# One constant product in place of three, and the second residual moved ahead of the second tile's gate, at the end of a feed-forward

## The chip, the cores and the metric

The kernel runs on one core of a Trainium2 chip. The metric is device microseconds of one execution; the lower, the better. The kernel before took 1181.12 us (median of three runs, 1177.47 to 1183.35).

## The reference

Two transformer blocks run one after the other on 256 rows of 1024 numbers, all in float32. The first block has two layers (an even and an odd one). In each, after the mixer:

```
h = x * (1.0 + sc_f) + sh_f
y = conv_ffn(h, w_up, conv_w, w_down)           # silu(gate) * val, 2816 wide
x = layer_norm(DN_ALPHA * x + (1.0 + g_f) * y, ln_ffn_g, ln_ffn_b)
```

`sc_f`, `sh_f` and `g_f` come from a second input `c` by a product with `ada_w`. The layer after it begins with `h = x * (1 + sc_m) + sh_m` and a product with its input weights. The second block (RMS norms, three attentions, a feed-forward 4096 wide) begins with `rmsnorm(x)` and a product with `w_in_2`.

The change lies at the two places where a feed-forward of the first block ends and the next layer begins. They are called turns here: the first turn (after feed-forward 0, towards the odd layer) and the second turn (after feed-forward 1, towards the second block).

## The kernel before, in words

The 256 rows are two tiles of 128 rows (`tt` 0 and 1); `x[:, tt, :]` is 128 x 1024. Every product of float32 matrices is made of three products of rounded parts (`product`, lines 1287 to 1289: high by high, high by low, low by high). The high part of a weight unit is made by ScalarE (`hi_unit`, line 849), the low part by GpSimd (`lo_unit`, line 733), and SyncE loads the next weights when a low part has been made.

The output of a feed-forward lies in four PSUM banks, 128 x 512 each: banks 0 and 1 are the two column halves of tile 0, banks 2 and 3 those of tile 1. TensorE finishes them in this order: the last three blocks' products of tile 0, then those of tile 1 (`downward` with `(0,)` and then `(1,)`).

VectorE has one queue, worked off in the order written. At the end of `ffn(f)` (lines 2237 to 2267) it does four kinds of work on each bank `j`:

- `gated(j)`, line 2249: multiply the bank by the gate row. It waits for bank `j` to be full; `gated(3)` waits for `down_done`, TensorE's very last product of the feed-forward.
- the residual, line 2261: `x = ALPHA * x + bank`; it needs its own `gated(j)` (`link.need(mark)`).
- the statistic of these 512 columns, line 2007 (`chunk_statistics`), and after the second bank of a tile `bn_aggr` (line 2267), which gives `var_ready` to GpSimd for the reciprocal square root (`power`, lines 745 and 747).

The order written is gated(0), gated(1), residual 0, statistic 0, gated(2), residual 1, statistic 1, aggregate of tile 0, gated(3), residual 2, statistic 2, residual 3, statistic 3, aggregate of tile 1.

First turn, after that. VectorE normalizes tile 0 (line 2029), builds eight columns of modulation from a bank of TensorE (`mod_columns`, lines 1942 to 1951), and normalizes tile 1. TensorE has meanwhile made 32 products of one column each (`mod_columns`, line 1486), waited for `gate_copied`, and run `keep_warm(3, 4)` (line 1395): three products of constants, 128 x 512, whose result nobody reads. In the trace each such float32 product is two records. Then it transposes x, eight blocks of tile 0 and eight of tile 1 (`transpose_rows`, line 1468; it waits for each tile's normalization). Bank `q` of the transposed x is full when both tiles' blocks `2q` and `2q+1` are in. ScalarE (line 892) and VectorE (line 1979) read it out into `h`, GpSimd makes most of the low part (line 772), and TensorE goes on with `first_units(2, ...)` (line 1424) and `second_unit` (line 1387).

Second turn. TensorE runs `keep_warm(11)`. VectorE does a whole layer norm (lines 2018 and 2021), ScalarE sums squares (line 1202), GpSimd raises to the power, VectorE scales (line 2058), and TensorE transposes `xn` and starts `first_units(4, ...)` (line 1425).

Of the kernel before, what the change touches and what calls it, by code (L numbers as in the profile page):

```python
# [108 lines left out]
def build(nc, W, consts, out):  # L109
# [156 lines left out]
    with ctx:  # L266
# [175 lines left out]
        def full(eng, name):  # L442

            b, _, k = turns[name]
            eng.wait_ge(bank_full[b], k)
            return bank[b]

        def evacuated(eng, name):

            b, k, _ = turns[name]  # L450
            eng.wait_ge(bank_free[b], k + 1)

        def free(name):

            return bank_free[turns[name][0]]
# [818 lines left out]
        def _(pe):  # L1274
# [117 lines left out]
            def keep_warm(n, b=6):  # L1392

                for _ in range(n):
                    nc.tensor.matmul(bank[b][:, :], ident, cst[:, 0:512], start=True, stop=True)
# [13 lines left out]
            def first_units(n, gs, rows=False, low_last=False):  # L1409
# [17 lines left out]
                def final(part, mm):  # L1427
                    g, _, w, i = part
                    if i == (TT if rows else w // P) - 1:
                        mm.then_inc(bank_full[4 + g % 2], 1)  # L1430
# [29 lines left out]
            def transpose_rows(n, src, ready=None):  # L1460

                o = [begin(("ht", n, q)) for q in range(4)]
                for tt in range(TT):
                    if ready is not None:
                        pe.wait_ge(row_ready, ready + tt)
                    for kt in range(KD):
                        c = S * (kt % 2) + P * tt
                        mm = nc.tensor.transpose(o[kt // 2][:, c:c + P], src[:, tt, P * kt:P * (kt + 1)], ident)
                        if tt == 1 and kt % 2 == 1:
                            done(mm, ("ht", n, kt // 2))  # L1470
# [238 lines left out]
            ffn(0)  # L1709
            mod_columns(1, (0,))  # L1710
            pe.wait_ge(gate_copied, 2)
            keep_warm(3, 4)
            transpose_rows(2, x, 3)
            first_units(2, G_Z[:1], rows=True)
            second_unit(G_Z[1], rows=True)
# [196 lines left out]
        def _(dve):  # L1912
# [92 lines left out]
            def chunk_statistics(tt, i, n):  # L2005

                return V.bn_stats(bnst[:, tt, 6 * i:6 * i + 6], x[:, tt, n * i:n * (i + 1)])
# [154 lines left out]
            def ffn(f, after_block=None):  # L2162
# [73 lines left out]
                def product_full(j):  # L2236

                    if j < 3:
                        full(dve, ("acc", f, j))
                    else:  # L2240
                        dve.wait_ge(down_done, d0 + nb)
                    return bank[j]

                def gated(j):

                    o = product_full(j)
                    if j < 2:
                        dve.wait_ge(gate_copied, 2 * f + j + 1)
                    return link.mark(V.tensor_tensor(o[:, :], o[:, :], grow[:, 1, 512 * (j % 2):512 * (j % 2 + 1)], ALU.mult))
# [6 lines left out]
                mark = gated(0)  # L2256
                for j, (tt, i) in enumerate(chunks):
                    c, o = slice(512 * i, 512 * (i + 1)), bank[j]
                    after = gated(j + 1) if j < 3 else None
                    link.need(mark)  # L2260
                    V.scalar_tensor_tensor(x[:, tt, c], x[:, tt, c], ALPHA, o[:, :], ALU.mult, ALU.add
                                           ).then_inc(free(("acc", f, j)), 1)
                    mark = after
                    evacuated(dve, ("acc", f, j))
                    link(chunk_statistics(tt, i, 512))
                    if i:
                        V.bn_aggr(mv[:, tt, :], bnst[:, tt, 0:12]).then_inc(var_ready, 1)


            dve.wait_ge(cond_exp, 1)  # L2270
# [95 lines left out]
            mod_columns(0, (1,), (0, 0))  # L2366
            h_columns(1, modT[:, 0, 24:32], modT[:, 0, 16:24])
            ffn(0, lambda b: restore_rows(1, 0, (b,)))
            normalize_rows(("ffn", 0), 1, (0,))
            mod_columns(1, (0,), (2, 0))  # L2370
# [59 lines left out]
            mod_columns(1, (1,), (0, 1))  # L2430
            h_columns(3, modT[:, 1, 24:32], modT[:, 1, 16:24])
            ffn(1, lambda b: restore_rows(3, 2, (b,)))
            layer_norm(("ffn", 1), 3)
            rms_rows(("rms",), D ** 0.5)
# [57 lines left out]
            rms_rows(("out2",), 1.0)  # L2492
            h_columns(5, mlp_gain, None)
            ffn(2)
            dve.wait_ge(ln_in, 32 * 4 + 16)
            for j in range(4):
# [33 lines left out]
```

## Time and profile before

| | |
|---|---|
| median of three runs | 1181.12 us |
| the profiled execution's own time | 1176.84 us |
| its span | 1175.0 us |
| TensorE busy | 1126.1 us (96%) |
| VectorE, ScalarE, GpSimd busy | 539.2, 590.9, 832.3 us |
| mean granted TensorE clock | 0.985 |
| `keep_warm`, line 1395 | 40 records, 372.6 to 981.0 us |
| `gated`, line 2249 | 8 instructions; idle before them 5.4 us in 4 waits for TensorE |

The busy times are sums over the whole span. The turns are short stretches: the first from some 363 to 392 us, the second from some 668 to 696 us. A row of the timeline gives start, length, engine, line and operation, what is written and read, and in square brackets the idle time of that engine before it and who ended it. Rows of one kind are merged: "x16" is sixteen of them, and the length is that of all.

### The profile page before, as it was taken

What the parts mean: (1) busy time and instruction counts of PE and PEld (TensorE: products, weight loads), DVE (VectorE), ACT (ScalarE), POOL (GpSimd) and SP (SyncE); (2) the same over time, 40 slices, a digit from 0 to 9 for tenths busy, and PEclk for the clock granted to TensorE, in tenths of its full rate; (3) what the DMA queues carried; (4) which work ended last, traced back from release to release, by engine and by line L of the source; (5) the groups of instructions that cost most, each with busy time, mean ns of one, the idle gap of its engine ahead of it and who ended that gap; (6) DMA issues with size and microseconds to landing.
All of it is one profiled execution on the core that took longest, in us unless ns stands there. A gap on an engine that the chain in (4) does not pass through costs nothing.

```text
span 1175.0 us, 21678 instructions
## 1 busy us (share of the span) xinstructions
PE 1126.1 (96%) x8119; PEld 1030.3 (88%) x8119; DVE 539.2 (46%) x1120; ACT 590.9 (50%) x894; POOL 832.3 (71%) x297
## 2 busy tenths in 40 slices
PE   5899999999999989999999989999999999999997
PEld 2799898999997978899999878999999988999996
DVE  4668877865656675783223441333111333111112
ACT  0455435454543564455545444555776543555444
POOL 3567569988785635888888746556656776988884
PEclk9899989999998999999999999999999999999999
DMA  9987798999985445697656315444444544666652
GB/s 337 320 270 205 249 289 276 337 321 327 308 294 188 133 126 181 188 292 217 195 171 204 108 46 181 133 128 130 139 144 144 190 151 144 204 190 186 189 180 88
DMA packets 253484, 238.03 MB, mean 203 GB/s; under 512 B 18075, under 2 KB 216528, under 8 KB 253424
## 3 DMA queue, kind: packets, MB, share of 16 engines
q1 hardware_dynamic: 235104, 198.70, 54.9%
q10 hardware_dynamic: 17712, 38.28, 9.1%
q8 instruction: 41, 0.67, 0.2%
q0 software_dynamic: 608, 0.22, 0.1%
q14 instruction: 19, 0.16, 0.0%
HBM read 236.12 MB, written 1.05 MB: 202 GB/s over the span
## 4 chain that ended last, share of the span: by engine, by line
PE 71%; DMA 8%; POOL 6%; ACT 6%; DVE 5%; issue 3%; SPq 1%; ACTq 0%; POOLq 0%; DVEq 0%
PE bank L1287 17%; PE bank L1288 17%; PE bank L1289 17%; POOL unit_lo L733 5%; PE bank L1312 3%; PE bank L1321 3%; PE bank L1313 2%; ACT unit_hi L849 2%; DMA raw<-in_ffn_w_up 2%; PE bank L1425 2%; DMA ada<-in_ada_w 1%; PE bank L1528 1%; PE bank L1348 1%; DMA raw<-in_ev_w_in 1%; DVE x L2044 1%
## 5 line engine op out<-in xcount | busy, mean ns | idle before, releaser
L733 POOL TENSOR_TENSOR unit_lo<-raw,unit_hi 128x2048 fp32r<-128x2048 f32 (+5 forms) x87 | 343.7, 3955 | 220.0 <-ACT unit_hi L849 219.2
L1287 PE MATMUL bank<-h_hi,unit_hi 128*128 128x256 f32 x1152 | 327.0, 284 | 0.0
L1288 PE MATMUL bank<-h_lo,unit_hi 128*128 128x256 f32 x1152 | 325.9, 283 | 0.0
L1289 PE MATMUL bank<-h_hi,unit_lo 128*128 128x256 f32 x1152 | 325.9, 283 | 0.0
L784 POOL TENSOR_TENSOR unit_lo<-raw,unit_hi 128x2048 fp32r<-128x2048 f32 (+1 forms) x70 | 257.0, 3672 | 75.1 <-ACT unit_hi L998 65.5
L1287 PEld LDWEIGHTS bank<-h_hi,unit_hi 128*128 128x128 f32 x1152 | 220.7, 192 | 5.3 <-issue 2.5
L1288 PEld LDWEIGHTS bank<-h_lo,unit_hi 128*128 128x128 f32 x1152 | 220.8, 192 | 2.5
L1289 PEld LDWEIGHTS bank<-h_hi,unit_lo 128*128 128x128 f32 x1152 | 220.8, 192 | 0.0
L849 ACT ACTIVATE unit_hi<-raw 128x2048 fp32r<-128x2048 f32 (+5 forms) x97 | 161.3, 1664 | 103.5 <-DMA raw<-in_ffn_w_up 27.3
L787 POOL TENSOR_TENSOR down<-raw_down,down 128x1024 fp32r<-128x1024 f32 x70 | 176.0, 2515 | 0.2 <-ACT down L1024 0.2
L2177 DVE SCALAR_TENSOR_TENSOR work<-bank,cols,work 128x254 f32<-128x254 f32 (+1 forms) x176 | 72.6, 473 | 129.3 <-ACT work L985 129.3
L1287 PE MATMUL bank<-down,y_hi 128*128 128x512 f32 x296 | 116.7, 394 | 3.5 <-DVE y_lo L2209 2.2
L1288 PE MATMUL bank<-down,y_hi 128*128 128x512 f32 x296 | 116.0, 392 | 0.0
L1289 PE MATMUL bank<-down,y_lo 128*128 128x512 f32 x296 | 115.3, 389 | 0.0
L998 ACT ACTIVATE unit_hi<-raw 128x2048 fp32r<-128x2048 f32 (+1 forms) x60 | 90.9, 1514 | 7.0 <-DMA raw<-in_ffn_w_up 6.0
L983 ACT ACTIVATE work<-bank,cols 128x256 f32<-128x256 f32 x44 | 20.8, 473 | 118.1 <-PE bank L1289 101.3
L2206 DVE TENSOR_TENSOR bank<-bank,work 128x256 f32<-128x256 f32 x32 | 13.8, 432 | 133.9 <-ACT work L988 133.9
L1024 ACT ACTIVATE down<-raw_down 128x1024 fp32r<-128x1024 f32 x60 | 63.4, 1056 | 14.4 <-PE bank L1289 14.3
L1312 PE MATMUL bank<-h_hi,unit_hi 128*128 128x256 f32 x272 | 69.7, 293 | 0.0
L1287 PEld LDWEIGHTS bank<-down,y_hi 128*128 128x128 f32 x296 | 55.8, 189 | 14.6 <-issue 4.9
L1313 PE MATMUL bank<-h_lo,unit_hi 128*128 128x256 f32 x272 | 67.8, 286 | 0.0
L1289 PEld LDWEIGHTS bank<-down,y_lo 128*128 128x128 f32 x296 | 55.6, 188 | 12.2
(363 smaller groups left out, 2180.4 us busy)
## 6 DMA issues: line engine op xcount, KB each, us to landing
raw<-in_ffn_w_up SPq DMA_DIRECT2D x86, 512.0 KB, 5.2
raw<-in_w_in SPq DMA_DIRECT2D x60, 512.0 KB, 4.6
raw_down<-in_ffn_w_down SPq DMA_DIRECT2D x44, 512.0 KB, 5.6
ada<-in_ada_w ACTq DMA_DIRECT2D x16, 1024.0 KB, 7.1
raw<-in_w_up SPq DMA_DIRECT2D x64, 256.0 KB, 3.1
raw_down<-in_w_down SPq DMA_DIRECT2D x32, 512.0 KB, 3.5
raw<-in_ev_w_in SPq DMA_DIRECT2D x28, 512.0 KB, 5.3
att<-in_ada_w ACTq DMA_DIRECT2D x14, 1024.0 KB, 8.0
```

The lines of the kernel that those rows point to most:

```text
L733: nc.gpsimd.tensor_tensor(ul[g % 2][:, w], raw_home(g)[:, w], uh[g % 2][:, w].bitcast(F32), ALU.subtract).then_inc(lo_up, 1)
L784: nc.gpsimd.tensor_tensor(ul[s][:, 0:w], raw[s][:, 0:w], uh[s][:, 0:w].bitcast(F32), ALU.subtract).then_inc(lo_up, 1)
L787: nc.gpsimd.tensor_tensor(down[:, 1 - k, 1, :], rawd[1 - k][:, :], down[:, 1 - k, 0, :].bitcast(F32), ALU.subtract).then_inc(lo_dn, 1)
L849: nc.scalar.activation(uh[s][:, w], raw_home(g)[:, w], ACT.Copy).then_inc(hi_up, 1)
L998: nc.scalar.activation(uh[s][:, 0:w], raw[s][:, 0:w], ACT.Copy).then_inc(hi_up, 1)
L1024: nc.scalar.activation(down[:, 1 - k, 0, :], rawd[1 - k][:, :], ACT.Copy).then_inc(hi_dn, 1)
L1287: nc.tensor.matmul(o, sh, mh, start=first, stop=False)
L1288: nc.tensor.matmul(o, sh, ml, start=False, stop=False)
L1289: return nc.tensor.matmul(o, sl, mh, start=False, stop=last)
L1312: nc.tensor.matmul(o[:, 0:S], uh[s][:, a], mh[:, kt, :], start=kt == 0, stop=False)
L1313: nc.tensor.matmul(o[:, 0:S], uh[s][:, a], ml[:, kt, :], start=False, stop=False)
L2177: return V.scalar_tensor_tensor(t[:, back:S], bank[4 + s][:, S * j:S * (j + 1) - back], w, t[:, back:S], ALU.mult, ALU.add)
```

## The change

Two edits. In `ffn` the product `gated(2)` is issued after the aggregate of tile 0 and not before residual 1, and `gated(3)` directly behind it. The order becomes gated(0), gated(1), residual 0, statistic 0, residual 1, statistic 1, aggregate of tile 0, gated(2), gated(3), residual 2, statistic 2, residual 3, statistic 3, aggregate of tile 1. This holds for both turns. In the first turn `keep_warm` runs one product of constants and not three.

```diff
@@ -1709,7 +1709,7 @@
             ffn(0)
             mod_columns(1, (0,))
             pe.wait_ge(gate_copied, 2)
-            keep_warm(3, 4)
+            keep_warm(1, 4)
             transpose_rows(2, x, 3)
             first_units(2, G_Z[:1], rows=True)
             second_unit(G_Z[1], rows=True)
@@ -2256,7 +2256,7 @@
                 mark = gated(0)
                 for j, (tt, i) in enumerate(chunks):
                     c, o = slice(512 * i, 512 * (i + 1)), bank[j]
-                    after = gated(j + 1) if j < 3 else None
+                    after = gated(j + 1) if j % 2 == 0 else None
                     link.need(mark)
                     V.scalar_tensor_tensor(x[:, tt, c], x[:, tt, c], ALPHA, o[:, :], ALU.mult, ALU.add
                                            ).then_inc(free(("acc", f, j)), 1)
@@ -2265,6 +2265,8 @@
                     link(chunk_statistics(tt, i, 512))
                     if i:
                         V.bn_aggr(mv[:, tt, :], bnst[:, tt, 0:12]).then_inc(var_ready, 1)
+                    if j == 1:
+                        mark = gated(2)
```

## Rows read from the trace of the kernel before

**Rows 1.** The page's chain that ended last, shares by engine.
```profile
PE 71%; DMA 8%; POOL 6%; ACT 6%; DVE 5%; issue 3%; SPq 1%; ACTq 0%; POOLq 0%; DVEq 0%
```

**Rows 2.** Timeline, VectorE, first turn: start, length, engine, line, operation, [idle before].
```profile
363.78 1.39 DVE L2249 TENSOR_TENSOR bank<-bank,gate_rows 128x512 f32<-128x512 f32 x2 [1.23 <-PE bank L1289]
...
365.79 0.69 DVE L2007 BATCH_NORM_STATS2 small<-x 128x6 f32<-128x512 f32 x1
367.96 0.70 DVE L2249 TENSOR_TENSOR bank<-bank,gate_rows 128x512 f32<-128x512 f32 x1 [1.48 <-PE bank L1289]
368.57 0.68 DVE L2261 SCALAR_TENSOR_TENSOR x<-x,bank 128x512 f32<-128x512 f32 x1
...
370.13 0.67 DVE L2249 TENSOR_TENSOR bank<-bank,gate_rows 128x512 f32<-128x512 f32 x1
370.72 0.67 DVE L2261 SCALAR_TENSOR_TENSOR x<-x,bank 128x512 f32<-128x512 f32 x1
...
375.32 0.81 DVE L2029 TENSOR_SCALAR x<-x,small 128x1024 f32<-128x1024 f32 x1 [0.18 <-POOL small L747]
```

**Rows 3.** Timeline, first turn: TensorE, then ScalarE, then GpSimd.
```profile
368.37 4.42 PE L1486 MATMUL bank<-consts,accg 128*128 128x1 f32 x32
372.65 5.38 PE L1395 MATMUL bank<-consts 128*128 128x512 f32 x6
377.88 1.91 PE L1468 MATMUL bank<-consts,x 128*128 128x128 f32 x16
...
385.74 1.22 PE L1424 MATMUL bank<-unit_hi,h_lo 128*128 128x256 f32 x8 [0.48 <-POOL h_lo L772]
...
379.23 1.02 ACT L892 ACTIVATE h_hi<-bank,cols 128x256 fp32r<-128x256 f32 x2 [13.74 <-PE bank L1468]
...
381.44 4.25 POOL L772 TENSOR_TENSOR h_lo<-h_full,h_hi 128x512 fp32r<-128x512 f32 x3 [6.23 <-DVE h_full L1979]
```

**Rows 4.** Stretches of 1 us, first turn; third number from the end: granted clock.
```profile
371.00:372.00 1.00, 1.00 (x6) 1.00 (x7) 0.96 (x2) 0.00 (x0) 0.18 (x1) 0.50 0.56 79
...
377.00:378.00 1.00, 1.00 (x4) 0.35 (x3) 0.00 (x0) 0.00 (x0) 0.00 (x0) 0.59 0.00 0
```

**Rows 5.** The odd mixer's end, without constant products: the timeline's transposes.
```profile
476.82 3.59 PE L1468 MATMUL bank<-consts,x 128*128 128x128 f32 x16 [0.21 <-DVE x L2029]
```

**Rows 6.** The same place: a stretch of 1 us with its granted clock.
```profile
480.00:481.00 1.00, 0.41 (x3) 0.06 (x1) 0.93 (x4) 0.29 (x1) 0.38 (x1) 0.89 1.08 371
```

**Rows 7.** Timeline, second turn: VectorE, then TensorE.
```profile
672.89 0.70 DVE L2249 TENSOR_TENSOR bank<-bank,gate_rows 128x512 f32<-128x512 f32 x1 [1.48 <-PE bank L1289]
...
684.29 0.75 DVE L2058 TENSOR_SCALAR att<-x,small 128x1024 f32<-128x1024 f32 x1 [0.53 <-POOL small L747]
...
685.92 0.75 DVE L2058 TENSOR_SCALAR att<-x,small 128x1024 f32<-128x1024 f32 x1 [0.87 <-POOL small L747]
...
673.30 9.60 PE L1395 MATMUL bank<-consts 128*128 128x512 f32 x22
...
685.20 3.51 PE L1468 MATMUL bank<-consts,att 128*128 128x128 f32 x16 [2.29 <-DVE att L2058]
```

**Rows 8.** Stretches of 1 us, second turn, with the granted clock.
```profile
685.00:686.00 1.00, 0.80 (x4) 0.83 (x5) 0.13 (x2) 0.00 (x0) 0.77 (x2) 0.51 0.00 0
...
688.00:689.00 1.00, 1.00 (x8) 1.00 (x8) 0.40 (x1) 1.00 (x4) 0.00 (x0) 0.78 0.00 0
```

**Rows 9.** Timeline, TensorE, the turn of the second block's output product.
```profile
983.13 1.09 PE L1468 MATMUL bank<-consts,att 128*128 128x128 f32 x8 [0.24 <-DVE att L2058]
985.75 0.36 PE L1425 MATMUL bank<-h_hi,unit_hi 128*128 128x256 f32 x1 [1.53 <-ACT h_hi L890]
```

**Rows 10.** The stretch of 1 us in which it stands idle there.
```profile
984.00:985.00 1.00, 0.22 (x3) 0.00 (x0) 0.40 (x1) 1.00 (x4) 1.00 (x1) 1.00 0.14 49
```

**Rows 11.** The chain that ended last, in order of time: start, length, what.
```profile
386.96 5.76 PE bank L1387 x48
...
462.62 0.37 SPq L665
463.03 5.30 DMA raw<-in_ffn_w_up
```

## Prediction

> **What bounds the kernel now.** I read the page first, for the chain that ended last: TensorE is 71% of it and VectorE 5% [rows 1], so an edit on VectorE pays only where TensorE waits for it, and one on TensorE pays wherever it sits. Then I read the timeline of each turn engine by engine, and the granted clock in stretches of 1 us.
>
> In the first turn VectorE stands idle 1.48 us before gated(2), waiting for bank 2, though residual 1 behind it in the queue needs nothing more [rows 2]. From there it runs without a real gap to the second normalization, which ends at 375.32 + 0.81 = 376.13. TensorE is later than that: its constant products run from 372.65 to about 377.88, and the transposes start on their heels [rows 3]. So in the first turn the constant products are the bound, by 1.75 us against x of tile 1 (377.88 - 376.13), and by more against tile 0. The clock explains why they are so long. The granted clock is 0.50 (1.2 GHz) from 371 us on, 2.6 us into the one-column products, and comes back to 2.4 GHz at about 377.8 (0.59 granted over 377 to 378) [rows 4]. Six records took 377.88 - 372.65 = 5.23 us, 0.872 each; at 2.4 GHz it is 9.60 / 22 = 0.436 [rows 3, 7].
>
> In the second turn TensorE has long finished its constant products (673.30 + 9.60 = 682.90) and waits 2.29 us for VectorE's scaled tile [rows 7]. There VectorE and its helpers are the bound, and the 1.48 us gap stands in front of their whole chain.
>
> **Edit 1, VectorE's order.** Nothing is added or removed, two products move. Before: the first statistic ends at 365.79 + 0.69 = 366.48, and residual 2 starts at 370.72, 4.24 us later [rows 2]. After: residual 1, statistic 1 and aggregate run at once; they take 370.13 - 368.57 = 1.56 us start to start, so from 366.51 to 368.07. Bank 2 was there at 367.96, so gated(2) doesn't wait. gated(3) follows; TensorE has gone on to its one-column products at 368.37 [rows 3], so bank 3 is full too, and two gates take 1.39 us less the 0.09 by which a residual starts inside the gate before it (367.96 + 0.70 against 368.57), 1.30 us; gated(3) comes at about 368.72 and doesn't wait either. Residual 2 starts at 368.07 + 1.30 = 369.37. **VectorE is 370.72 - 369.37 = 1.35 us earlier**, with everything behind it: second normalization done at 374.78. What is moved past what: gated(2) now stands behind statistic 1, which costs bank 2 about 0.1 us; nobody else waits for bank 2. GpSimd gets tile 0's variance some 2 us sooner, and nobody uses it before VectorE's own turn comes.
>
> In the first turn, as it stands, this edit alone would pay nothing, since TensorE comes later. With edit 2 it is a cover: see below.
>
> In the second turn the pattern repeats, gated(2) again idle 1.48 [rows 7], so the scaled tiles are ready at 684.29 + 0.75 - 1.35 = 683.69 and at 685.92 + 0.75 - 1.35 = 685.32. Transposes then start at 683.85 and not at 685.20. What follows hangs on the clock, which had fallen by 685 (0.51 granted) after 2.1 us of idleness, and was back near 688.4 (0.78 over that microsecond) [rows 8]. Lower bound: it falls again. Sixteen transposes at 3.51 / 16 = 0.219 us end at 687.36, then 1.08 us of products at half rate lose 0.54: the gain is 1.35 - 0.54 = 0.8. Upper bound: with TensorE idle for only 0.95 us (682.90 to 683.85) and 0.6 us between the tiles, the clock stays at 2.4 GHz, as it does over 1.53 us of idleness in another turn [rows 9, 10]. Then transposes take 1.09 / 8 = 0.136 at most, tile 1's run from 685.48 to about 686.5, and products start at 686.4 against 688.46: 2.05. I take **1.35**, near the middle; a low value and a high value are both one step of the clock away.
>
> **Edit 2, one constant product.** Four of six records go. If the clock runs as it did (half rate until 377.8), TensorE is through its constants at 372.65 + 2 x 0.872 = 374.4. Tile 0 is normalized by then, since VectorE is already at tile 1's normalization (375.32 - 1.35 = 373.97). Eight transposes at 0.219 end at 376.15, tile 1 has been ready since 374.78, eight more end at 377.9. Bank 0 is full after the tenth, at 374.4 + 2.19 = 376.6; before it was 377.88 + 10 x 0.119 = 379.07, and ScalarE started 0.16 us behind it [rows 3]. VectorE's first read waits for the twelfth transpose: 377.03 against 379.31, 2.28 earlier. GpSimd's three low parts hang on those reads, and TensorE waits 0.48 us for the last of them [rows 3]. From the earlier start of both (2.47 and 2.28), less a tenth or two for a bank that now comes in steps of 0.44 us, I take **2.15 us for the first turn**. Upper bound: the four records themselves, 3.5 us, if nothing else bound. Lower bound: if the clock happened to be full all along, TensorE would wait for tile 1's normalization on either side, and the gain would be edit 1's 1.35. Without edit 1 (tile 1 ready at 376.13 and TensorE there at 376.15) edit 2 would give the same 2.15 here: its cover is just gone, by 0.02.
>
> The constant products were there to bring the clock back. With one of them, the transposes must do it. That they can, the odd mixer's end shows: no constant products stand there, transposes run dense from 476.82 for 3.59 us, and the clock comes back inside 480 to 481 (0.89 granted), before any ordinary product [rows 5, 6]; the second turn shows the same [rows 7, 8]. A rule of the Trainium skill speaks against it: "TensorE: Matmul & The Clock Gate", section "Part 4: PE-mode transpose", says that transposes are not counted as activity that brings the full clock. These two places of the trace contradict it; it stands as a rival below.
>
> **Sum.** 2.15 + 1.35 = 3.5 us. Against the profiled execution's own 1176.84 us (span 1175.0 and 1.84 around it) that is 1173.3. That execution was 4.28 us below the median of the runs shown, 1181.12; on the median the sum gives 1177.6 us. I expect later work to keep the gain: the next weight transfer on the chain is issued by SyncE at 462.62, behind GpSimd's low part, and not by a stream that runs on its own [rows 11].
>
> **Rivals.**
> - *The clock's steps fall less well in both turns.* 1.35 + 0.8 = 2.15 us gained: 1179.0. For it: the steps of the clock do not follow the program, so each execution meets them elsewhere. Against it: nothing.
> - *The gain is given back.* A shift of 3.5 us is eaten by waits for weights, of which the chain has 8% DMA [rows 1]: 1181. Against it: the issue behind GpSimd [rows 11].
> - *Transposes don't count.* Then only ordinary products bring the clock back; with dense constants it took from 372.65 to 377.8, 5.1 us. Products from 377.9 on would be at half rate up to 383.0, losing 2.55 less the 0.48 of slack, so 2.1, and the first turn's 2.15 is gone. In the second turn the same from 687.36 to 692.4 loses 2.5 where the trace before lost nothing: 1.35 - 2.5 = -1.15. Together 1.1 us slower: 1182.2. This is what the Trainium skill's page named above would make of it. Against: rows 5 to 8.
> - *Slower: the clock stays at 1.2 GHz through the first units of the odd layer.* A constant product and transposes with short gaps could be too thin. 48 products of line 1424 and 48 of line 1387, 0.12 us each (5.76 / 48) [rows 11], at 0.24: from 377.9 to 400.9, against 392.72 before, 8.2 us later; with 1.35 from the second turn, 6.9 slower: 1188.0. It decides only if the clock comes back after about 387 us: 377.9 + 11.5 + half of the low time = 392.7 + 1.35. Against: it would have to ignore nine microseconds of dense products.
> - *The edit of the queue does nothing* (bank 2 comes before the statistic ends): excluded by 1.48 us idle, twice.
>
> **Chances.** Forecast 0.62, steps fall less well 0.14, given back 0.14, transposes don't count 0.04, low through the units 0.04, a larger gain than any counted here 0.02. About 0.5%, 5.9 us, is what a measurement can tell from no change. The forecast of 3.5 is below that; the three runs before span 5.9 us themselves, so medians can carry it across in a third of the forecast's cases: faster 0.21 with the larger gain, slower 0.05 with the last rival and a little scatter, the rest, 0.74, within. The range: the cases from 4.2 us gained (1176.9) to 1.1 lost (1182.2), widened by the scatter of medians below: 1172.0 to 1183.0.
>
> **What would show it.** In the profile after: VectorE without idle before the third gate product in both turns, its second normalization 1.35 us earlier against the first gate product; line 1395 with 2 records in the first turn; from the start of line 1486 to that of line 1387, 386.96 - 368.37 = 18.6 us before, 2.15 us shorter; in the second turn the transposes 1.35 us sooner after the feed-forward, idle before them about 0.95 and not 2.29, and the granted clock either 1.0 or 0.5 there. The clock must be back before or soon after the transposes of the first turn end. Wrong would be: a half clock in the products of lines 1424 and 1387 for over 3 us, or both turns shorter while the whole is not.

## The result and the profile after

The changed kernel takes 1171.64 us (median of nine runs, 1168.88 to 1174.22), the kernel before 1178.45 in the same set; the ratio is 0.9938 with a 95% interval of 0.9921 to 0.9956. That is 6.8 us faster, with an interval of some 5.2 to 9.3, and clear of no change. It was repeated three times: 0.9943 [0.9922, 0.9964], 0.9953 [0.9933, 0.9974], 0.9952 [0.9935, 0.9969]. Over all its 32 runs the changed kernel has a mean of 1171.7 us; 25 further runs of the unchanged kernel (x_before, y_before, z_before below) have 1177.6. So 5.9 us is the steadier number. One of the 12 runs of z_warm_only, below, took 1552.78 us at a granted clock of 0.652 and is left out of its ratio.

The forecast was 1177.6 us and the range ended at 1172.0. Part of the miss is the base: the first three runs of before had a median of 1181.12, the later ones lie near 1178. Against the profiled execution the sum gave 1173.3, and the profiled execution after took 1172.54 (span 1170.7). The rest is the effect itself, 5.9 to 6.8 where 3.5 was forecast.

The page's chain of after, which answers to [rows 1]: TensorE lost three points of the span.

```profile
PE 68%; DMA 8%; POOL 7%; DVE 6%; ACT 6%; issue 3%; SPq 1%; ACTq 0%; POOLq 0%; DVEq 0%
```

The timeline of VectorE in the first turn of after, which answers to [rows 2] (the last row is its first read of the transposed x):

```profile
363.58 1.39 DVE L2249 TENSOR_TENSOR bank<-bank,gate_rows 128x512 f32<-128x512 f32 x2 [1.23 <-PE bank L1289]
...
366.32 0.69 DVE L2261 SCALAR_TENSOR_TENSOR x<-x,bank 128x512 f32<-128x512 f32 x1
367.04 0.69 DVE L2007 BATCH_NORM_STATS2 small<-x 128x6 f32<-128x512 f32 x1
367.77 0.21 DVE L2267 BATCH_NORM_AGGREGATE small<-small 128x2 f32<-128x12 f32 x1
367.90 1.27 DVE L2249 TENSOR_TENSOR bank<-bank,gate_rows 128x512 f32<-128x512 f32 x2
369.08 0.68 DVE L2261 SCALAR_TENSOR_TENSOR x<-x,bank 128x512 f32<-128x512 f32 x1
...
373.68 0.81 DVE L2029 TENSOR_SCALAR x<-x,small 128x1024 f32<-128x1024 f32 x1 [0.18 <-POOL small L747]
375.91 1.45 DVE L1979 TENSOR_SCALAR h_full<-bank,cols 128x256 f32<-128x256 f32 x3 [1.41 <-PE bank L1468]
```

The pair of gate products has no idle time before it. Residual 2 starts 5.50 us after the first gate (369.08 - 363.58), before 6.94; the second normalization starts at 10.10, before 11.54. Both are 1.44 us earlier, where 1.35 was forecast.

TensorE's timeline and the granted clock of the same place, which answer to [rows 3] and [rows 4] (third number from the end: granted clock):

```profile
368.17 3.63 PE L1486 MATMUL bank<-consts,accg 128*128 128x1 f32 x32
371.66 1.31 PE L1395 MATMUL bank<-consts 128*128 128x512 f32 x2
373.00 3.32 PE L1468 MATMUL bank<-consts,x 128*128 128x128 f32 x16
```

```profile
371.00:372.00 1.00, 1.00 (x9) 0.94 (x9) 0.93 (x3) 0.00 (x0) 0.00 (x0) 1.00 0.81 119
372.00:373.00 1.00, 0.98 (x3) 0.03 (x1) 0.96 (x4) 0.00 (x0) 0.66 (x1) 0.71 0.99 347
...
375.00:376.00 1.00, 1.00 (x7) 1.00 (x6) 0.09 (x1) 0.53 (x2) 0.00 (x0) 0.58 0.00 0
```

The one-column products took 3.63 us and not 4.42, since the clock fell at 372.4 (8.8 us after the first gate) and not at 371.0 (7.2 us after it). It was back at 375.8, while the transposes were still running, and there was only one stretch at 1.2 GHz of 3.4 us. The transposes start 9.42 us after the first gate, and line 1387 at 19.65, before at 14.10 and 23.02.

The second turn, TensorE, which answers to [rows 7] and [rows 8]; first the timeline, then the stretch between the tiles:

```profile
680.32 1.07 PE L1468 MATMUL bank<-consts,att 128*128 128x128 f32 x8 [0.85 <-DVE att L2058]
681.86 1.09 PE L1468 MATMUL bank<-consts,att 128*128 128x128 f32 x8 [0.47 <-DVE att L2058]
683.01 0.35 PE L1425 MATMUL bank<-h_hi,unit_hi 128*128 128x256 f32 x1
```

```profile
681.00:682.00 1.00, 0.53 (x5) 0.30 (x4) 0.75 (x1) 0.00 (x0) 0.01 (x1) 1.00 0.00 0
```

TensorE is idle for 0.85 and 0.47 us, the clock stays at 2.4 GHz, sixteen transposes take 2.16 us in place of 3.51, and line 1425 starts 17.74 us after the turn's first gate (683.01 - 665.27), before 19.75.

### The profile page after: what moved, and what is told of

It reads as the page before. It is cut to its first block, busy times and chain, and to the rows that moved or that the text cites. A ratio compares the mean times of both kernels' runs of the same rounds, so it can differ in the third digit from the quotient of the medians.

```text
span 1170.7 us, 21670 instructions
## 1 busy us (share of the span) xinstructions
PE 1120.4 (96%) x8115; PEld 1026.8 (88%) x8115; DVE 538.4 (46%) x1120; ACT 590.6 (50%) x894; POOL 832.1 (71%) x297
## 3 DMA queue, kind: packets, MB, share of 16 engines
HBM read 236.12 MB, written 1.05 MB: 203 GB/s over the span
## 4 chain that ended last, share of the span: by engine, by line
PE 68%; DMA 8%; POOL 7%; DVE 6%; ACT 6%; issue 3%; SPq 1%; ACTq 0%; POOLq 0%; DVEq 0%
PE bank L1287 17%; PE bank L1288 16%; PE bank L1289 16%; POOL unit_lo L733 6%; ACT unit_hi L849 3%; PE bank L1321 2%; PE bank L1312 2%; PE bank L1313 2%; DMA raw<-in_ffn_w_up 2%; DMA raw<-in_ev_w_in 2%; DMA ada<-in_ada_w 1%; PE bank L1425 1%; DVE x L2044 1%; PE bank L1528 1%; DMA accg<-in_ada_w 1%
## 5 line engine op out<-in xcount | busy, mean ns | idle before, releaser
L1024 ACT ACTIVATE down<-raw_down 128x1024 fp32r<-128x1024 f32 x60 | 63.4, 1056 | 14.7 <-PE bank L1289 14.7
```

The lines of the kernel that those rows point to most:

```text
L1024: nc.scalar.activation(down[:, 1 - k, 0, :], rawd[1 - k][:, :], ACT.Copy).then_inc(hi_dn, 1)
```

## Stage lengths over all traces

Each kernel below left one trace. From each I read five places: the first gate of either turn, the first product of line 1387 and of line 1425, and the first of line 1528 (the scores of the next attention). "Constants" counts the constant products of the first turn, "new in" says in which turn VectorE has the new order, and "low" is how long the clock stood at 1.2 GHz in the first turn.

| trace | constants | new in | low, us | first turn | second turn | L1425 to L1528 |
|---|---|---|---|---|---|---|
| before | 3 | none | 6.8 | 23.02 | 19.75 | 43.03 |
| x_before | 3 | none | 6.8 | 23.01 | 19.18 | 43.38 |
| z_before | 3 | none | 6.8 | 23.00 | 19.64 | 43.37 |
| y_before | 3 | none | 3.4 | 21.34 | 19.77 | 43.36 |
| x_order_t2, y_order_t2 | 3 | second | 6.8, 3.4 | 22.99, 21.33 | 17.74, 17.73 | 43.05, 43.09 |
| x_order_t1, y_order_t1 | 3 | first | 3.4, none | 21.35, 19.66 | 19.64, 19.64 | 43.66, 44.03 |
| x_order_only, y_order_only | 3 | both | none, 6.8 | 19.64, 23.01 | 17.74, 17.72 | 43.05, 43.40 |
| x_warm_only, z_warm_only | 1 | none | 6.8, 6.8 | 21.08, 21.08 | 19.78, 19.70 | 42.14, 42.06 |
| after, x_after | 1 | both | 3.4, 3.4 | 19.65, 19.64 | 17.74, 17.74 | 42.38, 42.12 |
| z_after_a, z_after_b | 1 | both | 3.4, 3.4 | 19.62, 19.65 | 17.73, 17.72 | 42.05, 42.39 |
| x_warm0 | 0 | both | 6.8 | 19.64 | 17.75 | 42.25 |
| x_warm6 | 6 | both | 3.4 | 23.92 | 17.73 | 43.42 |
| z_pad2 | 1 and 2 tiny | both | 3.4 | 19.95 | 17.72 | 43.07 |
| z_three_nine | 3 | none | none | 20.50 | 19.64 | 42.82 |

## The experiments

**A control.** The unchanged kernel, three times; z_before was executed once only.

> The kernel before once more, unchanged, as a control and for a second trace of it. Stage lengths, from the first gate product of a turn to the first product of line 1387 (first turn) or line 1425 (second turn), were 23.0 and 19.8 us in the first trace. Theory A (the clock's low stretches do not follow the program): the second turn again 19.8, give or take half a microsecond; the first turn between 21.5 and 23.1, by whether its low stretch is 3.4 or 6.8 us long. Theory B (the trace shown was typical in every respect): 23.0 and 19.8 again, low stretch 6.8 us. Time within 0.2% of before either way.

> The kernel before, another control and a fourth trace of its first turn. With the clock's low stretch from 371 us for 6.8 us it was 23.0 in three traces. Theory A: below 23.0 where the low stretch is shorter or lies later, never below 21.0, which is 19.64 and the 1.35 of VectorE's idleness. Theory B: 23.0 always.

> The kernel before, one look for a further trace: first turn 23.0 where the low stretch is 6.8 us, 21.3 where it is 3.4, second 19.2 to 19.8.

Measured: 0.9994 [0.9976, 1.0011] and 0.9997 [0.9975, 1.0019]; the single execution of z_before, 1180.61 us, has no interval. The first turn is 23.0 in three traces and 21.34 in the fourth (y_before), where the clock fell 9.0 us after the first gate and not 7.2, for 3.4 us and not 6.8. The trace that the forecast rested on had the commoner, longer low stretch.

**The two halves.**

```diff
-            keep_warm(3, 4)          # x_warm_only, z_warm_only: this alone
+            keep_warm(1, 4)
```

> Edit 2 alone: one constant product and VectorE's old order. Theory A (in the first turn the cut alone lets TensorE run into the wait for tile 1, since with the clock back early VectorE's old order is late): first turn about 20.9 us, 1.3 longer than in the changed kernel, second turn 19.8 as before; in all 2.1 us faster than before. Theory B (the recorded step: edit 1 is covered by exactly nothing in the first turn, the cut alone gives what both give): first turn 19.7 as in the changed kernel, in all 3.4 us faster.

> One constant product, VectorE's old order, a second trace. Theory A (then VectorE is the bound in the first turn): first turn 21.0 to 21.1 again, 1.35 to 1.45 over the changed kernel; second turn 19.2 to 19.8; in all about 3.3 us slower than the changed kernel. The recorded step (the first turn's cover needs no new order): 19.7.

Measured: 0.9978 [0.9960, 0.9995] and 0.9984 [0.9968, 1.0001], so 2 to 2.6 us. The first turn is 21.08 in both traces, which is 1.44 over the changed kernel. TensorE then waits 0.72 us for VectorE's normalized tile 0, as the timeline of x_warm_only shows:

```profile
372.32 2.06 PE L1395 MATMUL bank<-consts 128*128 128x512 f32 x2
375.10 3.65 PE L1468 MATMUL bank<-consts,x 128*128 128x128 f32 x16 [0.72 <-DVE x L2029]
```

So the cut alone is worth 1.5 us of the first turn against the mean of the unchanged kernel's four traces (22.59 - 21.08), and the rest of the turn's gain needs edit 1. The recorded step (edit 2 would give the same without edit 1) is refuted. Both kinds of time agree: the cut alone gains 2 to 2.6 us, both edits 5.9.

```diff
-                    after = gated(j + 1) if j < 3 else None       # x_order_only: this alone
+                    after = gated(j + 1) if j % 2 == 0 else None
...
+                    if j == 1:
+                        mark = gated(2)
```

> Edit 1 alone: VectorE's new order, three constant products. Theory A: the second turn 17.7 us as in the changed kernel (clock stays full over the shorter wait), the first turn between 21.5 and 23.1 by its low stretch, since the constant products still end last; 2.0 us faster than before, up to 3 where the low stretch is short. Theory B (the second turn's full clock in the changed kernel was luck): second turn 18.4 to 19, in all 1.0 to 1.4 faster.

> The new order in both turns, three constant products, a second time. Theory A: 3.5 to 5 us faster than before, second turn 17.7, first 19.6 to 21.4. Theory B: 1.9 us faster, first turn 23.0 in this trace. If it is again 5.8 faster and the first turn alone again nothing, the two turns do not add, and something that the stage lengths do not hold is at work.

Measured: 0.9951 [0.9931, 0.9970] and 0.9971 [0.9953, 0.9990]. The two first turns are as far apart as they can be. In x_order_only the clock never fell, and in y_order_only it fell early. The first's 19.64 lies below the 21.5 to 23.1 of its expectation, and its 5.8 us above the 1.0 to 3 there; the second's 23.0 is what theory B said of it, and its 3.4 us lies near theory A's 3.5 to 5. The timelines of the two, x_order_only first (TensorE, then VectorE):

```profile
371.26 2.82 PE L1395 MATMUL bank<-consts 128*128 128x512 f32 x6
373.92 1.91 PE L1468 MATMUL bank<-consts,x 128*128 128x128 f32 x16
...
373.28 0.81 DVE L2029 TENSOR_SCALAR x<-x,small 128x1024 f32<-128x1024 f32 x1 [0.19 <-POOL small L747]
375.50 0.99 DVE L1979 TENSOR_SCALAR h_full<-bank,cols 128x256 f32<-128x256 f32 x2 [1.41 <-PE bank L1468]
```

```profile
366.86 4.82 PE L1486 MATMUL bank<-consts,accg 128*128 128x1 f32 x32
371.54 4.97 PE L1395 MATMUL bank<-consts 128*128 128x512 f32 x6
376.34 1.91 PE L1468 MATMUL bank<-consts,x 128*128 128x128 f32 x16
```

The same three products take 2.82 us in the one and 4.97 in the other. At 1.2 GHz they are the bound, and the new order is hidden. At 2.4 GHz they end 10.90 us after the first gate, just as tile 1 is normalized (10.91), but tile 0's eight transposes stand behind them and start at 10.74 where after starts them at 9.42. VectorE's first read of the transposed x comes at 12.32 us in x_order_only (375.50 - 363.18) and at 12.33 in after (375.91 - 363.58), whose transposes ran at 1.2 GHz. So the 19.64 of both is a coincidence of two different bounds. One constant product, the new order and a clock that never falls is a case that no trace here shows.

**The new order in one turn only.**

```diff
+                    after = gated(j + 1) if j % 2 == 0 or (f != 0 and j < 3) else None   # t1; t2: f != 1
...
+                    if j == 1 and f == 0:                                                 # t2: f == 1
+                        mark = gated(2)
```

> VectorE's new order in the first turn only; second turn and the three constant products as before. The recorded step says: no gain at all, since the constant products end last (0.0 us, first turn 23.0). Theory A: the first turn's length goes with the clock. Where TensorE stays at 2.4 GHz the constant products are over 2.7 us after the one-column products and the new order pays all of itself, 19.6 us; where the clock is at 1.2 GHz for 6.8 us from 371 on, they are the bound and it stays 23.0. The median of the runs then lies 1 to 3 us below before; second turn 19.2 to 19.8.

> VectorE's new order in the first turn alone, a second time, together with its two neighbours on one chip, since the first set does not add up: the new order in the first turn gave nothing (0.9999), in the second turn 3.2 us, in both 5.8. Theory A (the first turn's order is worth 1.4 to 3.4 us by the clock, and the first set's 0.9999 was scatter): 1.5 us or more faster than before, first turn 19.6 to 21.4. Theory B (with three constant products it is worth nothing on the average, the recorded step): within 0.8 us of before.

> VectorE's new order in the second turn only; first turn as before with three constant products. Both theories: the second turn 17.7 us, 1.5 to 2.0 less than before; the first between 21.0 (full clock) and 23.0 us. In all 1.7 us faster by the stage lengths. Rival C (something beyond the turns shortens with either edit): over 2.5 us faster.

> The new order in the second turn alone, a second time. Both theories: second turn 17.7 us against 19.2 to 19.8 with the old order, 1.9 us faster in all (1 to 3 by the median); first turn 21 to 23.0.

Measured: in the first turn alone 0.9999 [0.9982, 1.0016] and 0.9993 [0.9974, 1.0012], so less than Theory A said both times and no gain that can be told. In the second alone 0.9973 [0.9955, 0.9991] and 0.9981 [0.9963, 1.0000]: 2.2 to 3.2 us (rival C had asked for over 2.5), and in both traces the second turn is 17.7. With three constant products, edit 1 is worth its second turn and next to nothing in its first, on the average; the recorded step holds there. In x_order_t1 three constant products at 1.2 GHz were again the bound (21.35, as 21.34 in y_before with the old order). The two single ones sum to some 3.2 us and both together gave 3.4 and 5.8; with intervals of 2 us to either side nothing speaks against a plain sum.

**How many constant products.** `keep_warm(0, 4)` and `keep_warm(6, 4)` in the changed kernel.

> The changed kernel without any constant product in the first turn. Theory A (constants are neither the bound nor needed, VectorE's normalization of tile 1 is the bound at 10.9 us after the first gate product): first turn 19.6 to 20.3 us, in all within 1 us of the changed kernel. The rival that constant products bring the clock back (transposes don't count): the first units of the odd layer at 1.2 GHz for some microseconds, first turn over 21 us, 1.5 us or more slower than the changed kernel.

> The changed kernel with six constant products in place of one: the slope of a constant product where it is surely the bound. From their start at 8.1 us after the first gate product, 6 x 0.872 = 5.2 us at 2.4 GHz or 10.5 at 1.2 GHz, then 8.9 us to line 1387: first turn 22.2 us at full clock, up to 27 at half clock. Theory A: 22.2 to 24, in all 2.6 to 4.5 us slower than the changed kernel. If constant products mattered as predicted at the low clock only (2 x 0.872 each): 27, 7.5 slower.

Measured: without any 0.9945 [0.9927, 0.9963], as the changed kernel. The clock was at 1.2 GHz from 372.3 to 379.1 in this trace, and the first turn is still 19.64. TensorE waited 1.20 us for tile 0 and started its transposes 9.42 us after the first gate, as in after:

```profile
373.34 3.65 PE L1468 MATMUL bank<-consts,x 128*128 128x128 f32 x16 [1.20 <-DVE x L2029]
```

```profile
372.00:373.00 1.00, 0.14 (x2) 0.05 (x1) 0.96 (x3) 0.00 (x0) 0.40 (x1) 0.67 0.82 251
...
379.00:380.00 1.00, 1.00 (x10) 1.00 (x10) 0.74 (x3) 1.00 (x3) 1.00 (x2) 0.92 0.00 0
```

With six, 1.0004 [0.9987, 1.0021]: 6.6 us slower than the changed kernel, first turn 23.92 in the trace. Five more products cost 4.3 us in the trace's turn (23.92 - 19.64), and 1.2 in the stretch from line 1425 to line 1528 (below). Theory A's 2.6 to 4.5 held for the turn and was too small for the times.

**The changed kernel again.**

> The changed kernel once more, unchanged, to be compared with the two halves on the same chip. Theory A: 5.4 us faster than before (3.4 in the first turn and 2.0 in the second), first turn 19.6, second 17.7. Theory B (the first trace had two lucky clocks): 3.5 us faster, first turn 20.9, second 18.4. Rival C: 6.8 us faster because something beyond the two turns is shorter too, with stretches outside the turns shorter by over 1 us in this trace.

> The changed kernel, a third trace. Theory A (VectorE's normalization of tile 1 is the bound whatever the clock does): first turn 19.64, second 17.74, the stretch between them 282.0, times 4.6 to 5.4 us below before. Theory D (the first turn is 19.64 only where the clock falls late): 20.9, as the recorded sum had it, where the low stretch starts before 371.5 us. Rival C (more than the turns): the parts outside the turns shorter than before's by 1 us or more in both new traces.

> The same kernel as z_after_a, a fourth trace, with the same expectations: 19.64 and 17.74 by theory A, 20.9 in the first turn by theory D where the low stretch starts early.

Measured: the ratios of the first section. In four traces the first turn is 19.62 to 19.65 and the second 17.72 to 17.74. Theory D was not put to the test: in none of the four did the clock fall as early as in the trace of before (8.8 to 9.5 us after the first gate, against 7.2). Rival C came true in part: from line 1425 to the end, the mean of the four is 485.2 us against 487.0 in the four traces of the unchanged kernel.

**The stretch behind the second turn.** From line 1425 to line 1528 it is 43.0 us or more in all eleven traces with three or six constant products and the second turn's eleven, and 42.05 to 42.4 in all seven with one or none, though the edit lies 350 us ahead of it. A load of `w_in` stands on the chain. The chain of before, then of z_after_a, in order of time (start, length, what):

```profile
714.35 0.37 SPq L616
714.76 5.82 DMA raw<-in_w_in
720.60 1.92 ACT unit_hi L849
```

```profile
709.08 0.37 SPq L616
709.49 4.87 DMA raw<-in_w_in
714.38 1.92 ACT unit_hi L849
```

The same transfer takes 0.95 us less. The two last runs ask whether TensorE's number of instructions does it.

```diff
             keep_warm(1, 4)                         # z_pad2
+            for _ in range(2):
+                nc.tensor.matmul(bank[4][:, 0:8], ident, cst[:, 0:8], start=True, stop=True)
```

```diff
-            keep_warm(11)                           # z_three_nine, on the kernel before
+            keep_warm(9)
```

> The changed kernel with two products of eight columns beside the one constant product: as many TensorE instructions as with three, but not their time. All theories: first turn 19.6, second 17.7 us. Theory E (instruction count, by where instruction loads fall): the stretch from line 1425 to line 1528 is 43.0 us or more, as with three constant products, and the time about 1 us above the changed kernel's 1171.7. Theory F (the time shift or chance): 42.1 to 42.4.

> The kernel before (old order, three constant products in the first turn) with nine in place of eleven constant products in the second turn, where TensorE waits for VectorE anyhow. First turn 21.3 or 23.0; second 19.2 to 19.8. Theory E: from line 1425 to line 1528 42.1 to 42.4 us, since TensorE's stream is two products shorter by then, and the time up to 1 us below before. Theory F: 43.0 to 43.7, time as before.

Measured: z_pad2 0.9985 [0.9972, 0.9997], median 1175.08, which is 3.4 us above the changed kernel's 1171.7, for two products of eight columns. By the ratios, each against the kernel before of its own set, it is more: 1.8 us gained, where the changed kernel gained 5.5 to 7.3. The expectation had said about 1 us. Its stretch is 43.07, and the transfer is long again; its chain:

```profile
710.24 0.37 SPq L616
710.65 5.97 DMA raw<-in_w_in
716.65 1.93 ACT unit_hi L849
```

z_three_nine 0.9988 [0.9975, 1.0002], stretch 42.82, between what the two theories said. Its transfer, though, is as short as in the kernels with a short stretch:

```profile
713.42 4.79 DMA raw<-in_w_in
```

What made its stretch 42.82 lies ahead of the loads: its clock was still at 1.2 GHz for the first 1.3 us of line 1425, and the first load of the stretch is issued 14.7 us behind the start of line 1425, not 14.1. Without these 0.6 us it is 42.2, in the range of theory E. So in all 20 traces this load takes 5.8 to 6.3 us or 4.7 to 5.1, and which of the two goes with the number of products that TensorE was given before: long in the eleven traces with three or six constant products and in z_pad2, short in the seven with one or none and in z_three_nine.

The traces also show where the load of instructions falls, a packet of 16 KB of queue q8 (kind "instruction"). It starts at 717.34 in before, 2.6 us into the transfer of 714.76 to 720.58, and at 713.53 in z_after_a, 4.0 us into that of 709.49 to 714.36. Over all traces it is 2.6 to 3.1 us into the transfer in eleven of the twelve long ones (0.9 in x_warm6), and 4.0 to 4.5 in all eight short ones. That the number of instructions moves this packet against the weights is thus seen; why its place is worth 1 us is not.

z_three_nine also gives the old order with three constant products and a clock that never fell in the first turn: 20.50. My expectation for y_before had said never below 21.0; that was wrong, since at 2.4 GHz the transposes are faster as well. It is one trace.

## Why the prediction was wrong

The measured time lies below the range, and a gain larger than any that was counted had been given 0.02. What failed is the first turn's term, the second turn's middle value, and "later work keeps the gain", which put everything behind the turns at nothing. By its own steps:

- **Edit 1, VectorE 1.35 us earlier:** right, 1.44 in both turns, and no wait before either gate.
- **Second turn, 1.35 taken between 0.8 and 2.05:** the mechanism was right and the value wrong. It is near the upper bound in every trace with the new order: 17.72 to 17.75 in eleven, against 19.18 to 19.78 in nine with the old one, 1.9 on the average (2.01 in the first pair). Of this 1.44 is the order; in x_before, where the clock did not fall in spite of the 2.29 us, the old order has 19.18. TensorE idle 0.85 and 0.47 us never let the clock fall; I had halved between two cases of which one did not happen in eleven.
- **First turn, 2.15:** the mis-sized term. The first pair of traces gives 3.37. The step assumed that the clock would fall at the same place and come back at 377.8. In after it fell at 372.4 and came back after 3.4 us, so the one-column products lost nothing, the constant product took 1.31 us, and the normalization of tile 0 was the bound, with the transposes behind it, at 19.64. The forecast's 20.87 (23.02 - 2.15) was never seen. Over the four traces each the gain is 22.59 - 19.64 = 2.95, since one old trace had 21.34.
- **How much of the 2.95 is luck:** this stays open. Up to the end of the one-column products, 8.2 us after the first gate, TensorE does the same work in both kernels, and the clock of before fell at 7.2 us, so the edits of this turn can't be seen to have moved it. Against y_before, whose clock fell at 9.0 for 3.4 us much as in after, the gain is 21.34 - 19.64 = 1.70. An early fall (6.8 to 7.2 us) came in five of the eleven traces with three constant products and in none of the nine with fewer, with six or with the tiny ones. What the changed kernel takes after an early fall no trace shows, so 2.15 is not refuted for the state that it was priced in; that this state would come again is what failed.
- **"Its cover is just gone, by 0.02":** wrong. Without edit 1 the first turn is 21.08 (twice), 1.44 more. The step compared TensorE with tile 1 alone. VectorE's timeline of before has tile 0 normalized at 374.49 (373.73 + 0.76, below), after the 374.4 of the sum, and in x_warm_only TensorE waits 0.72 us for tile 0.

```profile
373.73 0.76 DVE L2029 TENSOR_SCALAR x<-x,small 128x1024 f32<-128x1024 f32 x1
```

- **"As it stands, edit 1 alone would pay nothing in the first turn":** right on the average (0.9999, 0.9993), wrong where the clock stays up (19.64 and 19.66, against 20.50 with the old order).
- **Transposes bring the clock back:** right. In the second turn of before TensorE ran nothing but transposes from 685.20 until line 1425 started at 688.46, and the clock, which was at 1.2 GHz, came back at 688.4. x_warm0 does not decide it: its clock rose at 379.1 us, behind sixteen transposes and 2 us of products of line 1424, at no cost to the turn. The rule of the Trainium skill ("TensorE: Matmul & The Clock Gate", "Part 4: PE-mode transpose"), which speaks against it, is contradicted by the second turn of before.
- **Later work keeps the gain:** too little, a term put at nothing. The sum ended at the turns: 2.95 and 1.85, so 4.8 us by four traces each. Another 1.05 comes from line 1425 to line 1528 (43.28 against 42.24), the load of `w_in` above; two tiny products take it back, so it belongs to the change, though not to the work that the change saves. And 1.1 comes right behind it: before has the clock at 1.2 GHz from about 736 to 740 us in all four traces (in z_before from 740.0 to 743.4), and after only in one of four. That part of the attention, from line 1528 to line 1547, takes 14.95 us with it and 13.45 without. Ten of all 20 traces have it, among them x_order_only but not y_order_only, the same kernel. These terms make 7.0; the traces' spans differ by 7.6, the means of all runs by 5.9. Most of what the spans have over the terms comes from z_before alone, which was also at 1.2 GHz from 446.4 to 453.3 us and took 284.8 us from line 1387 to the second turn's first gate, where the other three took 281.9 to 282.1. Four traces each can't settle the last microsecond, and how much of the 1.1 belongs to the change and how much to how the clock happened to fall stays open.

Stretches of 1 us of before there (third number from the end: granted clock), with 0.61 and 0.50:

```profile
736.00:737.00 1.00, 1.00 (x5) 0.80 (x4) 1.00 (x5) 1.00 (x6) 1.00 (x1) 0.61 0.31 107
...
738.00:739.00 1.00, 1.00 (x7) 1.00 (x6) 0.96 (x5) 0.74 (x5) 0.90 (x1) 0.50 0.00 0
```

No run beats the changed kernel; zero constant products and one are the same within the interval.

## What to carry to other kernels

A gap on an engine that is not the bound may still be worth closing, if it stands before a wait of TensorE: the shorter wait can keep the clock up, which here paid some 0.5 us on top of 1.44 in the second turn. Filler products meant to keep TensorE busy cost nothing while they end before the first tile comes (one product or none gave the same 19.6); here three of them and the new order gave 19.64, 21.35 or 23.0 us in the first turn, by where the clock fell, and one of them 19.6 in all four traces. So size them for the low clock, and take two or three traces before pricing them, since one trace shows one state of the clock. Where two engines arrive close to each other, an edit on one is in part hidden by the other: in the first turn the new order alone paid nothing that could be told, the cut alone 1.5 us, and with the cut in place the new order paid 1.44. And check each of the tiles that an engine waits for, not the last one alone.

## What was not expected of the hardware

- The same stage of the same kernel has discrete lengths: 23.0 or 21.3 us in the first turn with three constant products, and where the clock never falls 20.5 with the old order and 19.6 with the new, repeating to 0.04 us within a state.
- Two products of eight columns, far from the bound, moved the whole by 3.4 us (1171.7 to 1175.1), with 1.0 us of it in a weight transfer 340 us later (4.9 against 6.0 us), where a load of instructions starts earlier within the transfer. Where the other 2.4 us lie stays open. A comparison of 0.3% between kernels with unlike instruction counts can hold an effect of this size that has nothing to do with the work.
